# Token rows to expert slots by an indirect DMA through DRAM, in place of a 0/1 product per pair of experts

## What is computed

```python
def hier_moe(h, wg, bg, we, be, w1, w3, w2):
    x = h.reshape(-1, D)
    ...                                  # top-1 group of 4, then top-2 experts of its 4
    comb = jnp.einsum('nk,nke->ne', wts, jax.nn.one_hot(ids, N_EXPERTS, dtype=jnp.float32)).astype(x.dtype)
    h1 = jnp.einsum('nd,edf->nef', x, w1)      # 1024 -> 512
    h3 = jnp.einsum('nd,edf->nef', x, w3)
    a = jax.nn.silu(h1) * h3 * comb[:, :, None]
    return jnp.einsum('nef,efd->nd', a, w2).reshape(B, T, D)
```

## Time and profile before

| | |
|---|---|
| median of 3 runs | 889.7 us (888.27 to 891.15) |
| the profiled execution, time | 890.58 us |
| its span, first to last instruction | 888.8 us |
| TensorE busy | 823.3 us, 93% |
| VectorE, ScalarE, GpSimd busy | 35%, 23%, 1% |
| moved by DMA | 277.33 MB, 312 GB/s over the span |
| experts of layer 0, first `up` to last `down` | 230.9 to 469.4 us |
| experts of layer 1, first `up` to last `down` | 628.8 to 867.3 us |

### The profile page before, as it was taken

The page is one execution under the profiler, slowest core; times in us unless marked ns, Lnnn a source line. Parts: engine busy times, 40 slices in busy tenths (PEclk is TensorE's granted clock), DMA queues, the critical chain, the costliest instruction groups (busy, mean ns, idle before and its releaser), DMA issues.

```text
span 888.8 us, 11017 instructions
## 1 busy us (share of the span) xinstructions
PE 823.3 (93%) x4377; PEld 427.9 (48%) x4377; DVE 308.7 (35%) x663; ACT 204.5 (23%) x430; POOL 7.5 (1%) x10
## 2 busy tenths in 40 slices
PE   3899989998999999999996999998999999999992
PEld 1554535544545544545542657544545544544441
DVE  0305076125522243324227212235422334224217
ACT  2301555116211211112112301116211211112110
POOL 0000000001000000000000000001000000000000
PEclk9899999999999999999997999999999999999996
DMA  9796799726499999999947932027399999999931
GB/s 375 254 422 253 272 427 409 312 94 237 170 392 431 403 409 401 423 413 401 420 194 312 430 111 96 0 94 284 128 390 425 409 404 406 431 406 405 402 167 72
DMA packets 26430, 277.33 MB, mean 312 GB/s; under 512 B 7517, under 2 KB 8433, under 8 KB 9489
## 3 DMA queue, kind: packets, MB, share of 16 engines
q1 hardware_dynamic: 26033, 275.22, 75.7%
q10 hardware_dynamic: 288, 1.34, 0.4%
q0 software_dynamic: 64, 0.13, 0.0%
HBM read 274.99 MB, written 1.70 MB: 311 GB/s over the span
## 4 chain that ended last, share of the span: by engine, by line
PE 88%; DVE 4%; ACT 2%; DMA 2%; DVEq 1%; issue 1%; ACTq 0%; SPq 0%
PE bank L1668 25%; PE bank L1684 13%; PE bank L1661 10%; PE bank L1596 9%; PE bank L1838 6%; PE bank L1692 5%; PE bank L1967 4%; PE bank L1537 4%; DMA ring<-in_ada_w 2%; PE bank L1674 2%; DVEq L1035 1%; PE bank L1988 1%; PE bank L1906 1%; PE bank L1576 1%; PE bank L1885 1%
## 5 line engine op out<-in xcount | busy, mean ns | idle before, releaser
L1668 PE MATMUL bank<-ring,Z 128*64 128x512 f32 x1024 | 226.1, 594 | 1.4 <-ACT Z L961 1.4
L1668 PEld LDWEIGHTS bank<-ring,Z 128*64 128x64 f32 x1024 | 71.9, 137 | 140.3 <-issue 138.6
L1684 PE MATMUL bank<-ring,Z 128*64 128x512 f32 x512 | 113.4, 595 | 2.5 <-issue 1.3
L1661 PEld LDWEIGHTS bank<-Z,h 128*128 128x128 f32 x768 | 88.0, 192 | 27.1 <-issue 22.7
L1661 PE MATMUL bank<-Z,h 128*128 128x128 f32 x768 | 93.7, 279 | 2.8 <-DVE Z L1126 2.8
L1596 PE MATMUL bank<-ring,T 128*128 128x512 f32 x192 | 83.1, 592 | 1.2 <-ACT T L1001 1.2
L1248 DVE COPY Z<-bank 128x512 f32<-128x512 f32 x28 | 19.4, 691 | 184.3 <-PE bank L1661 184.3
L1684 PEld LDWEIGHTS bank<-ring,Z 128*64 128x64 f32 x512 | 36.2, 137 | 70.8 <-issue 69.1
L1692 PE MATMUL bank<-ys,Cs 128*128 128x512 f32 x192 | 53.5, 424 | 16.2 <-DVE Z L1336 10.4
L1260 DVE SCALAR_TENSOR_TENSOR ys<-bank,row_weight,ys 128x512 fp32r<-128x512 f32 x32 | 22.6, 749 | 117.5 <-ACT ys L947 117.5
L931 ACT ACTIVATE Z<-bank 128x512 f32<-128x512 f32 x32 | 19.1, 597 | 188.7 <-PE bank L1668 188.7
(11 more groups left out here) (216 smaller groups left out, 657.7 us busy)
## 6 DMA issues: line engine op xcount, KB each, us to landing
ring<-in_moe_w SPq DMA_DIRECT2D x94, 2048.0 KB, 12.5
ring<-in_ada_w SPq DMA_DIRECT2D x24, 2048.0 KB, 13.1
ring<-in_a_w_in SPq DMA_DIRECT2D x2, 2048.0 KB, 21.8
ring<-in_a_w_out SPq DMA_DIRECT2D x2, 2048.0 KB, 12.5
ring<-in_moe_w SPq DMA_DIRECT2D x4, 1024.0 KB, 11.7
ring<-in_f_w_in SPq DMA_DIRECT2D x2, 2048.0 KB, 19.9
ring<-in_f_w_out SPq DMA_DIRECT2D x2, 2048.0 KB, 28.6
special<-in_att_const SPq DMA_DIRECT2D x1, 1792.0 KB, 7.8
```

The lines of the kernel that those rows point to most:

```text
L1661: last = pe.matmul(psX[q][:, k * w:(k + 1) * w], h[:, t, kk * P:(kk + 1) * P], Sel[:, t, 0:w], start=(t == 0), stop=(t == NT - 1))
L1668: last = pe.matmul(psU[BLK * q:BLK * (q + 1), :], xT[:, b, k, s0:s0 + BLK], w[:, k, :], start=(k == 0), stop=(k == KT - 1), skip_group_che ...
L1684: last = pe.matmul(psD[hh][BLK * u:BLK * (u + 1), :], aT[:, u, k, :], w2[:, k, HALF * hh:HALF * (hh + 1)], start=(k == 0), stop=(k == FC - ...
```

## The change

The token rows no longer come out of a product. After routing, GpSimd writes each token's row of `h` twice, to the two slots that it has, into a DRAM buffer `slot_rows`, by six indirect DMAs (3 tiles, 2 choices; 128 rows of `ROW` = 1032 numbers, 4128 bytes, each). When all six have landed it reads the slots back in blocks of 128 rows, one plain DMA of 528,384 bytes per pair, into `xg` (two buffers); the block for pair p ≥ 2 waits for DVE's `slots_read` of pair p-2. PE turns a block with 8 transposes by the identity (`turn_rows`) in place of 24 products (48 in the trace's count). The product with `Sel` stays for the first pair of each layer alone, since its rows are needed before a trip through DRAM could be over.

Each row carries 8 more numbers: its two slots, two weights, and its token number. From these DVE makes `row_weight` and `Cs` directly (`slots_read`: four small operations, one of them 128x384), so `weighted`, `CT`, `combine_rows` and the two ACT operations on `psC`, Sign among them, are gone. A slot that holds no row of this layer must have weight 0: slots are numbered with 4096 added in layer 1, and in layer 0 ACT first fills `slot_rows` with zeros by one DMA of 14 x 128 rows (7.4 MB), issued at the start of `norm_ffn_act(0)`.

The hardware loops over pairs are written out. `back` of the pair before, six products in a row so far, is split: three after `up` of expert 1, three after the second `middle`. SBUF tensors are laid out by hand in one slab.

```diff
+                gp.wait_ge(slots_known, l + 1)
+                for t in range(NT):
+                    for a in range(2):
+                        gp.indirect_dma_start(slot_rows[:, :], bass.IndirectOffsetOnAxis(ap=slot_i[:, a, t:t + 1], axis=0),
+                                              row_of[:, t, :], None).then_inc(rows_out[l], 16)
+                gp.wait_ge(rows_out[l], 16 * 2 * NT)
+                for p in range(NPAIR):
+                    if p >= 2:
+                        gp.wait_ge(pairs[l]["slots_read"], p - 1)
+                    gp.dma_start(xg[:, p % 2, 0:ROW], slot_rows[p * P:(p + 1) * P, 0:ROW]).then_inc(rows_in[l][p % 2], 16)
...
             def norm_ffn_act(l):
+                if l == 0:
+                    act.wait_ge(zero_rows, 1)
+                    zeros = ys[:, :, :].bitcast(F32).rearrange("p a n -> p (a n)")[:, 0:ROW].unsqueeze(1)
+                    act.dma_start(slot_rows.rearrange("(b p) n -> p b n", p=P), zeros.to_broadcast([P, ROW_TILES, ROW]))\
+                       .then_inc(slots_cleared, 16)
...
                 slots_of_tokens()
-                dve.tensor_tensor(c12, c12, bc(p1.unsqueeze(1), 2, NT), ALU.mult)
-                settle()
-                weighted(pairs[l], 0, 2 * BLK)
+                dve.tensor_copy(slot_i[:, :, :], G12)
+                columns = lambda a, b: row_of[:, :, D + a:D + b].rearrange("p t a -> p a t")
+                dve.tensor_scalar(columns(0, 2), G12, float(l * LAYER_SLOTS), None, ALU.add)
+                dve.tensor_copy(columns(4, 8), bc(con("token").unsqueeze(1), 4, NT))
+                dve.tensor_tensor(columns(2, 4), c12, bc(p1.unsqueeze(1), 2, NT), ALU.mult).then_inc(slots_known, 1)
...
+                def slots_read(s, b, w):
+                    m = xg[0:w, b, D:D + 5]
+                    dve.scalar_tensor_tensor(slot_weight[0:w, :], m[:, 0:2], slot_id[0:w, :], m[:, 2:4],
+                                             ALU.is_equal, ALU.mult)
+                    dve.tensor_scalar(Cs[0:w, b, :], con("iota")[0:w, :], m[:, 4:5], None, ALU.is_equal)
+                    settle()
+                    dve.tensor_reduce(row_weight[0:w, b:b + 1], slot_weight[0:w, :], AX.X, ALU.add)\
+                       .then_inc(s["slots_read"], 1)
...
+                def turn_rows(q, b, s):
+                    for k in range(4):
+                        kk = 4 * q + k
+                        last = pe.transpose(psX[q][:, k * P:(k + 1) * P], xg[:, b, kk * P:(kk + 1) * P], ident)
+                    last.then_inc(s["gathered"], 1)
...
+                    def next_rows():
+                        pe.wait_ge(rows_in[l][1 - b], 16 * ((p + 1) // 2 + 1))
+                        pe.wait_ge(s["x_cols"], p * 2 + 2)
+                        if p >= 2:
+                            pe.wait_ge(s["back_out"], taken + 4)
+                        for q in range(2):
+                            turn_rows(q, 1 - b, s)
...
+                    up(s, b, 0, weights(0, KT), weights(1, KT))
+                    if last:
+                        backs(0, NT)
+                    elif not first:
+                        next_rows()
...
+                    middle(s, 0)
+                    up(s, b, BLK, weights(2, KT), weights(3, KT))
+                    if last:
+                        backs(NT, 2 * NT)
+                    elif not first:
+                        backs(0, NT)
...
+                    middle(s, 1)
+                    if first:
+                        next_rows()
+                    elif not last:
+                        backs(NT, 2 * NT)
```

More of the change, by code:

```diff
@@ L403, in build @@
     with ctx:
+        slab_at = (nc.sbuf_base + 31) // 32 * 32
+        slab = (nc.sbuf_usable_end - slab_at) // 32 * 32 - 64
+        ctx.enter_context(nc.sbuf_tensor("slab", [P, slab // 4], F32))
+        start, end = {}, [slab_at]
         def sb(name, shape, dt=F32):
-            return ctx.enter_context(nc.sbuf_tensor(name, shape, dt))
+            start[name] = end[0]
+            n = int(np.prod(shape[1:])) * (2 if dt == BF16 else 4)
+            end[0] += (n + 31) // 32 * 32
+            assert end[0] <= slab_at + slab, (name, end[0] - slab_at - slab)
+            return nc.alloc_sbuf_tensor_at(name, shape, dt, offset=start[name])
         def sem(name):
@@ L578, in build @@
         zeroed = sem("zeroed")
+        zero_rows = sem("zero_rows")
+        slots_cleared = sem("slots_cleared")
+        slots_known = sem("slots_known")
+        rows_out = [sem(f"rows_out_{l}") for l in range(L)]
+        rows_in = [[sem(f"rows_in_{l}_{b}") for b in range(2)] for l in range(L)]
         normed = sem("normed")
@@ L610, in build @@
                  "act_cols",
-                 "comb_full",
-                 "comb_out",
+                 "slots_read",
                  "down_full",
@@ L618, in build @@
         pairs = [{k: sem(f"{k}_{l}") for k in steps} for l in range(L)]
-        overs = [{k: sem(f"over_{k}_{l}") for k in steps + ("weights", "done")} for l in range(L)]
+        overs = [{k: sem(f"over_{k}_{l}") for k in steps + ("weights", "rows", "done")} for l in range(L)]
         block = ctx.enter_context(nc.Block())
@@ L714, in _ @@
                     expert(u, k, w)
[L715 to L730 removed]
+                for p in range(1, NPAIR):
+                    for k, (u, w) in enumerate(items[:5] if p == NPAIR - 1 else items):
+                        sp.wait_ge(*last_use(n0 + 6 * p + k - NS))
+                        expert(2 * p + u, 6 * p + k, w)
+                last = n0 + 6 * NPAIR - 1
+                sp.wait_ge(*last_use(last - NS))
+                src, dst = moe_w2[l, NE - 1], ring[:, last % NS, :]
+                sp.dma_start(dst[:, 0:SLOT // 2], src[:, 0:SLOT // 2]).then_inc(arrived[last % NS], 16)
                 sp.dma_start(dst[:, SLOT // 2:], src[:, SLOT // 2:]).then_inc(late_half, 16)
@@ L740, in _ @@
                             sp.wait_ge(o["done"], j + 1)
+                            sp.wait_ge(rows_out[l], 16 * 2 * NT)
+                            sp.wait_ge(s["slots_read"], NPAIR)
+                            sp.dma_start(xg[0:BLK, 0, 0:ROW], slot_rows[bass.ds(j * BLK + NE * BLK, BLK), 0:ROW])\
+                              .then_inc(o["rows"], 16)
                             ex = sp.value_load(plan_i[0:1, bass.ds(j, 1)], min_val=0, max_val=NE - 1)
@@ L1293, in moe @@
                 dve.wait_ge(s["gathered"], 2)
-                pair(s, 0, 0, first=True)
-                pair(s, 1, 1)
-                with dve.Fori(1, NPAIR // 2 - 1) as i:
-                    for b in range(2):
-                        pair(s, i * 2 + b, b)
-                pair(s, NPAIR - 2, 0)
+                for p in range(NPAIR - 1):
+                    pair(s, p, p % 2)
                 last = NPAIR - 1
@@ L1315, in moe @@
                         with dve.If(j < blocks):
-                            select(o, 0, BLK)
+                            dve.wait_ge(o["rows"], j * 16 + 16)
+                            slots_read(o, 0, BLK)
                             for q in range(2):
@@ L1675, in middle @@
                     last.then_inc(s["mid_full"], 1)
-                def combine_rows(s, b, w):
-                    for t in range(NT):
-                        last = pe.transpose(psC[0:w, t * P:(t + 1) * P], CT[:, b, t, 0:w], ident)
-                    last.then_inc(s["comb_full"], 1)
                 def down(k, hh, ws):
@@ L1764, in moe @@
                 gather(1, 2 * BLK, s)
-                pair(0, 0, 0, first=True)
-                pair(1, 1, 1)
-                with pe.Fori(1, NPAIR // 2 - 1) as i:
-                    for b in range(2):
-                        pair(i * 2 + b, i * 2 + b, b)
-                pair(NPAIR - 2, NPAIR - 2, 0)
-                pair(NPAIR - 1, NPAIR - 1, 1, last=True)
+                for p in range(NPAIR):
+                    pair(p)
                 pe.wait_ge(plan_ready, l + 1)
```

194 lines of the change are left out of this document (82 added, 112 removed).

## The result

| | before | after |
|---|---|---|
| median of the runs | 889.8 us (4 runs, 888.3 to 891.2) | 907.7 us (4 runs, 904.7 to 908.8) |
| ratio | 1 | 1.0197, 95% interval 1.0166 to 1.0228 |
| profiled execution | 890.6 us, span 888.8 | 906.9 us, span 905.1 |

The change makes the kernel slower by 2.0%. The forecast was 886.5 with a range up to 901: it has the wrong sign, and the time lies outside the range.

What follows compares the result with a forecast made beforehand. PE was taken as the bound, DMA 1.4 us per pair behind and the bound afterwards. Stream and tail save 7.1 us, less 2 x (0.5 + 1.3) for the start: 3.5 off 889.7, rounded to 886.5 us; range 882 to 901.

Steps and rivals of the forecast that it cites:

- The ceiling and the period: Expert stages: DMA moves at most 431 GB/s, so a pair with its row block lasts 30.4 us.
- row traffic is free: Rival, expert stages: row traffic in its own queue doesn't slow the weights; 867 us, chance 0.02 shared with one other case.
- DMA follows PE: Rival, expert stages: DMA keeps PE's pace, needing 486 GB/s; 824 us, chance 0.02 shared with one other case.
- PE has time to spare: Expert pairs: PE needs 25.9 us against DMA's 30.4, so it waits 4.5 us per pair.
- The tail: End of each layer's experts: the last `down` ends 7.4 us after the last landing; 3.8 and 5.9 us saved.
- The clearing: Zero fill of `slot_rows`, issued about 162: costs nothing, 17 us at most.
- the clock: Rival, each pair's first `up`: wholly at half speed, 14.0 us for 7.0; 921 us, chance 0.03.
- The issue of an indirect write: Start of each layer's experts, GpSimd: 1.1 us per write, bounded by 0.67 and 2.66.
- what the start costs: Start of each layer's experts: 0.5 us for writes and 1.3 us for the late `down`, per layer.
- own sign of being wrong: Pair 0: a PE wait for rows of 10 us or more would show the forecast wrong; 2 to 6 expected.
- `down` ends at 270 to 273, dry for 10 to 12 us: Upper bound at the start, pair 0: with writes of 2.66 us, rows land at 262 and the weight stream runs dry.
- rival (a): Start of each layer's experts stalls with indirect writes of about 2 us: 5 us slower per layer, 900 us; chance 0.28.

Runs made afterwards that it cites:

- the last kernel: Against the kernel with the product in pairs 1, 3, 5, 7: indirect writes carry only 8 numbers; plain DMA stores token rows, indirect reads gather pairs 2, 4, 6; 870.4 us.

## Why the prediction was wrong, step by step

What held:

- **The ceiling and the period.** Forecast 425 to 431 GB/s and pairs of 30.4 us; measured 427 GB/s and 30.6 (342.66 to 373.30), or 29.4 where no row block is read (403.94 to 433.30). The rivals "row traffic is free" and "DMA follows PE" are out.
- **PE has time to spare.** Forecast were 4.5 us per pair. In the stretch of three pairs shown above PE is busy for 82.44 of 90.64 us: 2.7 us per pair, less than forecast (PE's pair is 27.5 us, not 25.9, partly by `up`s that ran for 8.8 us), but enough for DMA to set the pace. PE's busy time fell by 46 us and not by the 60 forecast: all `up`s together take 236.7 us (226.1 before) and all `back`s 61.4 (53.5).
- **The tail.** Forecast 7.4 us from the last landing to the end of `down`. The row of the last half matrix (L748) and the last `down` give it:

```profile
L748 SPq DMA_DIRECT2D ring<-in_moe_w x2: 432/432/432, 452.0 to 855.4; - x2
...
DMA to landing us min/median/max: 20.4/20.4/20.4
```

```profile
472.75 7.09 PE L1726 MATMUL bank<-ring,Z 128*64 128x512 f32 x32 [0.93 <-DVE Z L1284]
```

  452.0 + 20.4 is 472.4, and `down` ends at 479.84: 7.4 us, as it said, against 11.2 before.
- **The clearing** costs nothing that shows, and **the clock** nothing in the later pairs: an `up` that ran partly at 1.2 GHz, after 2.4 us of waiting (granted 0.80 over it, 8.8 us for 7.1), lay within that slack.
- **The issue of an indirect write.** Taken at 1.1 us; it is 0.95 to 1.01, one every 1.26 us or so, so that the last leaves GpSimd at 239.3 and not at 236.6, 1.3 us of this by the later stage.

What failed is the term **what the start costs**, 1.8 us per layer (0.5 for the writes + 1.3 for the late `down`). The prediction's own sign of being wrong, a wait in pair 0 of 10 us or more, came with 17.7. Forecast for the stage were 237.8 and 235.7 us (238.5 less 2.5 and 4.6, plus 1.8); measured 247.6 and 246.0. That is 9.8 and 10.3 us over, together 20.1, all of the miss: 890.6 - 3.5 + 20.1 gives 907.2 beside the 906.9 of the profiled execution. With the 1.8 the start cost 11.6 and 12.1 us. Two sizes in it were wrong, with one cause:

1. The last write was to land near 240, 2.3 us for a small one and 1.2 for the bytes. It landed at 250.0. The first weights of pair 1 go out at 239.3, so the queued writes move beside them. Alone it is there 4.5 us after its issue (239.3 to 243.8), beside 4 KB pieces 7.6, beside 8 KB 9.1, beside 16 KB 11.6 (14.1 in the kernel with the product for pair 1, whose first write kept GpSimd for 1.69 us and pushed the others back).
2. The reads were priced by the one DMA in the trace that ran beside weights, 130 GB/s, 8 us and up to 12. They took 15.6 us. The rows of that DMA are 6.4 KB, and I scaled by the length as an upper bound only; the share of a queue is its row against the other's piece, and for the second block 88 GB/s is left.

So rows came in at 266.7 instead of 250 to 254. The point at which the stream runs dry, 262.1, was nearly right (the rate falls from 427 GB/s to 45 between 264 and 266, in a stage that began 1.3 us later), and the bound "`down` ends at 270 to 273, dry for 10 to 12 us" was the case that came true, at 277. I had tied that bound to writes of 2.66 us, and rival (a), the start that stalls, to "1.5 us per write". That condition was wrong: the writes are short, and the price lies in the landing. The time of rival (a), 900, had the right sign and was still 8 us short.

The 0.5 us charged for the writes was small as well: the last kernel, which takes their row data out, has stages shorter by 1.7 and 2.3 us. It differs in its reads too, so this is an estimate.

The kernel with the product for pair 1 confirms the rest of the sum. It has two row blocks fewer per layer, 4 x 1.23 = 4.9 us, so with them it would be at 880.3 + 4.9 = 885.2, against the forecast's 886.5: had the start cost what was assumed, the forecast would have stood within a microsecond or two.

Open: the start of a layer's first `up` in layer 0 varied between 228.7 and 233.2 us over the kernels, though nothing ahead of it was changed in most of them; why, I did not find out. It moves a profiled execution by up to 4 us, but not the stages, which are compared here.

## What to carry to other kernels

Rows of 4128 bytes that start beside a stream of loads with larger pieces got here a share by the ratio of their row to the other's piece, and not an equal one: price such transfers by that ratio, and look at what stands behind them on the waiting engine. A wait costs only where it keeps buffers from being freed and the stream runs dry; so put the work that frees buffers ahead of it, or let the first consumer take another way, as the product did for pair 1. And where one engine has slack and another is at its ceiling, do the dear step both ways in turn instead of replacing it everywhere.

## What the runs showed of the hardware that I had not expected

- Two blocks of 128 rows of 4128 bytes land in 3.6 and 5.0 us alone, and in 10.3 and 15.6 us beside loads with 16 KB for each partition; the same loads cut to 4 KB pieces make it 7.1 and 8.9 us, and the total rate stays at 412 GB/s in the stretch shown.
- An indirect write of 128 rows keeps GpSimd for 0.95 to 1.03 us, whether its rows have 32 or 4128 bytes (the row below has 32); a few took longer, up to 1.70 us:

```profile
L805 POOL DMA_INDIRECT slot_rows<-h,slot_i x6: 958/962/1027, 227.9 to 234.3; - x6
```

- Reading back 512 rows of 32 bytes beside the weights took 6.4 to 7.4 us in the last kernel, about as long as 128 rows of 4128 bytes beside 4 KB pieces.
